# FFN input product of a two-layer transformer block: paired weight steps, so that matmuls of one width stand in runs of four steps in place of two

## The chip, the cores and the metric

The kernel runs on one core of a Trainium2 chip. The metric is the device time of one execution in microseconds (us). The profiled execution is one more execution, recorded by the hardware profiler.

## What is computed

Two decoder layers on 256 tokens of width 2048 in float32: attention mixers (left as they are by the change) and, in each layer, a feed-forward part whose first product is the subject:

```python
def conv_ffn(h, w_in, conv_w, conv_b, w_out):      # h: 256 x 2048, D_FF = 5632
    u = h @ w_in                                   # 2048 x 11264
    up = jnp.pad(u, ((0, 0), (CONV_WIDTH - 1, 0), (0, 0)))
    c = conv_b
    for j in range(CONV_WIDTH):
        c = c + conv_w[j] * up[:, j:j + s]
    g, val = c[..., :D_FF], c[..., D_FF:]
    return (jax.nn.gelu(g, approximate=True) * val) @ w_out
```

## The kernel before, in words

**High and low halves.** Float32 products are made from two parts of each operand, a rounded high part and the rest, the low part: high x high, high x low and low x high are added up in PSUM. For weights, ScalarE (ACT in rows) writes the high part `w_hi` from the landed weights `w_raw` (line 1315), and VectorE (DVE) then writes the low part `w_lo` (line 1903). I write hi(k) for TensorE's eight matmuls of step k with `w_hi`, and lo(k) for the eight with `w_lo`.

**Steps and slots.** A weight step is one load of 128 x 1024 weights (512 KB). `w_raw`, `w_hi` and `w_lo` have R = 4 slots each; step s uses slot s % 4. TensorE waits for `lo_ready` before a step, that is, for its low part (and so its high one, which VectorE reads). ScalarE may write the high part of step s once TensorE has added one to `step_used` for step s - 4. SyncE loads step s once `lo_ready` has come for step s - 4.

**Tiles.** In each layer the product is cut into 22 tiles of 512 output columns, by turns of the gate half and of the value half, with DSTEPS = 8 steps each. Even tiles use PSUM banks 0 to 3, odd ones banks 4 to 7. `merged_product` issues a tile: `both_halves` makes 8 matmuls of 512 columns (`w_hi` against both parts of x), `high_half` makes 8 of 256 columns (`w_lo` against the high part of x). Even steps go hi, lo; odd steps lo, hi. Tile 0 of a layer also carries transposes between its steps; tiles 1 to 20 are issued in a loop (line 1071), two in each turn, and tile 21 behind it.

**Epilogues.** While TensorE works on tile n, ScalarE and VectorE finish tile n - 1 in the gaps between splits, in an order written out by hand and the same in each loop turn: after the split of step 2 ScalarE copies PSUM (line 1704) as soon as the tile's last matmul is done, VectorE adds and scales it (lines 2413, 2415), and after the split of step 3 ScalarE makes the first convolution tap (line 1712); after the split of step 4 VectorE adds the other taps (line 2427, eight instructions), and the split of step 5 stands behind them. A gate half then gets its gelu (line 1721). Behind a value half, gate times value (line 2437) follows the split of step 5, the high part of the result `hT_hi` (line 1727) and its low part `hT_lo` (line 2443) follow that of step 6, and the splits of step 7 and of the next tile's step 0 stand behind them. So a tile during which a gate half is finished (odd tiles) and one during which a value half is finished (even tiles) differ; below they are the odd and the even tiles.

Of the kernel before, what the change touches and what calls it, by code (L numbers as in the profile page):

```python
# [22 lines left out]
P = 128  # L23
# [8 lines left out]
S = 256  # L32
# [17 lines left out]
R = 4  # L50
# [5 lines left out]
DSTEPS = KC // 2  # L56
LSTEPS = LORA // P // 2
FSTEPS = FC // 2
FJ = F // 512
# [89 lines left out]
def val(const, per, i):  # L149

    return const if i is None else i * per + const


def program(nc, x_in, mem_in, positions, inv_freq, w, vec, out):

    with ExitStack() as ctx:
        sem = lambda name: ctx.enter_context(nc.semaphore(name))
        base = 16512

        def at(name, shape, dt, offset):  # L160
            return nc.alloc_sbuf_tensor_at(name, shape, dt, offset=base + offset)
# [5 lines left out]
        xT = at("xT", [P, 2, KC, S], F32R, XT0)  # L167
        xT_hi, xT_lo = xT[:, 0], xT[:, 1]
        w_raw = at("w_raw", [P, R, 1024], F32, RING0)
        w_hi = at("w_hi", [P, R, 1024], F32R, RING0 + 16 * KB)  # L170
        w_lo = at("w_lo", [P, R, 1024], F32R, RING0 + 32 * KB)
# [120 lines left out]
        ps = ctx.enter_context(nc.psum_tensor("ps", [P, 8, 512], F32))  # L292
# [14 lines left out]
        step_used = sem("step_used")  # L307
# [192 lines left out]
        def _(pe):  # L500
            def release(tile_no, per=0, i=None):

                if tile_no >= 2:
                    pe.wait_ge(pair_act, val(tile_no - 1, per, i))
                    pe.wait_ge(pair_dve, val(tile_no - 1, per, i))
# [53 lines left out]
                    if turn_done:  # L559
                        turn_done(k, part_no)  # L560

            def merged_product(s0, tile_no, base, per=0, i=None, per_t=0, late=(), after=None):


                release(tile_no, per_t, i)
                for k in range(DSTEPS):
                    pe.wait_ge(lo_ready, val(s0 + k + 1, per, i))
                    for step, semaphore, value in late:
                        if k == step:
                            pe.wait_ge(semaphore, value)  # L570
                    slot = (s0 + k) % R
                    blocks = [(c, m4, slice(512 * c + P * m4, 512 * c + P * (m4 + 1)))
                              for c in range(2) for m4 in range(4)]
                    end = k == DSTEPS - 1

                    def both_halves(stop):
                        for c, m4, cols in blocks:
                            mm = nc.tensor.matmul(  # L578
                                ps[:, base + m4, :].rearrange("p (a n) -> p a n", a=2),
                                w_hi[:, slot, cols], xT[:, :, 2 * k + c, :], start=k == c == 0,  # L580
                                stop=stop and c == 1, skip_group_check=True)
                        return mm

                    def high_half(stop):
                        for c, m4, cols in blocks:
                            mm = nc.tensor.matmul(ps[:, base + m4, S:2 * S], w_lo[:, slot, cols],  # L586
                                                  xT_hi[:, 2 * k + c, :], start=False,
                                                  stop=stop and c == 1, skip_group_check=True)
                        return mm

                    if k % 2 == 0:
                        both_halves(False)
                        mm = high_half(end)
                    else:
                        high_half(False)
                        mm = both_halves(end)
                    mm.then_inc(step_used, 1)
                    if after:
                        after(k)

            whole = lambda n: (lambda a: a[:, 0:n])
            every = slice(0, S)
# [58 lines left out]
            def phase_free():  # L661

                if done["N"]:
                    pe.wait_ge(tr_lo, done["N"])
                if done["C"]:
                    pe.wait_ge(tr_copied, done["C"])
                if items_done[0]:
                    pe.wait_ge(o_lo, items_done[0])
# [20 lines left out]
            def x_transpose(g, tiles):  # L689

                return plain_transpose(x, g, tiles)

            def token_row(diag_no):

                pe.wait_ge(diag_ready, diag_no)
                pe.wait_ge(consts_ready, 2)
                nc.tensor.matmul(ps[:, 4, 0:S], ones[:, :],
                                 diag[:, :, :].rearrange("p t n -> p (t n)"), start=True,
                                 stop=True, skip_group_check=True).then_inc(tr_ready, 1)
# [11 lines left out]
            def unrotated_transpose(bank, buffer, rows, raw_no):  # L711

                pe.wait_ge(raw_ready, raw_no)
                for t in range(TT):
                    mm = nc.tensor.transpose(ps[:, bank, P * t:P * t + rows],
                                             pe_raw[0:rows, buffer, P * t:P * (t + 1)],
                                             ident[0:rows, 0:rows])
                mm.then_inc(unrotated, 1)
# [171 lines left out]
            def keep_busy(n, bank=WARM_BANK, block=ident_b[:, :]):  # L890

                for _ in range(n):
                    nc.tensor.matmul(ps[:, bank, 0:P], block, block, start=True, stop=True,  # L893
                                     skip_group_check=True)
# [74 lines left out]
            def beside_second(k):  # L969
# [3 lines left out]
                if k >= DSTEPS:  # L973
# [8 lines left out]
                    late=[(k, None, tr_lo, base_n + k + 1) for k in range(DSTEPS)])  # L982
# [5 lines left out]
                    after=lambda k: k == 1 and unrotated_transpose(6, 0, P, 1))  # L988
# [3 lines left out]
            for j in range(6):  # L992

                product(UQ + j * LSTEPS, LSTEPS, UQ_T + j, latq_hi, latq_lo, uq_parts(), width=384,
                        after=lambda k: k == 0 and j > 0 and
# [44 lines left out]
            def ffn_in(s_in, t_in, pieces, diag_no):  # L1040

                phase_free()
                pe.wait_ge(x_piece, pieces + 1)
                for g in range(4):
                    x_transpose(g, [0])
                pe.wait_ge(pair_act, t_in - 1)
                pe.wait_ge(pair_dve, t_in - 1)
                keep_busy(24, 2 * (t_in % 2))
                for g in range(4):
                    if g % 2 == 0:  # L1050
                        pe.wait_ge(x_piece, pieces + 3 + g // 2)
                    x_transpose(g, [1]).then_inc(tr_ready, 1)
                keep_busy(18, 2 * (t_in % 2))
                base_n = done["N"]
                done["N"] += DSTEPS
                done["C"] += 1
                tiles = lambda j, **kw: merged_product(s_in + j * DSTEPS, t_in + j, 4 * (j % 2), **kw)

                def between(k):
                    if k == 0:  # L1060
                        pe.wait_ge(x_piece, pieces + len(FFN_PIECES))
                    if k < 4:
                        x_transpose(4 + k, range(TT)).then_inc(tr_ready, 1)
                    if k == DSTEPS - 2:
                        token_row(diag_no)

                pe.wait_ge(pair_act, t_in)
                pe.wait_ge(pair_dve, t_in)
                tiles(0, late=[(k, tr_lo, base_n + k + 1) for k in range(DSTEPS)], after=between)
                pe.wait_ge(tr_copied, done["C"])  # L1070
                with pe.Fori(0, FJ - 1) as i:
                    for j in (1, 2):
                        tiles(j, per=2 * DSTEPS, i=i, per_t=2)
                tiles(2 * FJ - 1)

                h_count[0] += FJ
                pe.wait_ge(h_lo, h_count[0] - 1)

            pe.wait_ge(e_ready, T0_B - 2)
            for j in range(4):  # L1080
                product(OA + j * DSTEPS, DSTEPS, OA_T + j, xT_hi, xT_lo, n_parts(),
                        first_chunk=MEM_CHUNK, hold=HOLD if j % 2 else 0,
                        after=None if j else beside_oa0,
                        late=() if j else [(0, None, o_lo, T0_B - 7), (1, None, o_lo, T0_B - 3),
                                           (DSTEPS - 2, None, o_lo, T0_B - 2),
                                           (DSTEPS - 1, None, o_lo, T0_B)])
            ffn_in(IN0, IN0_T, PIECES_IN0, 4)

            def skv_transposes(k, part):
# [7 lines left out]
            for j in range(4):  # L1097
                product(OUT0 + j * FSTEPS, FSTEPS, OUT0_T + j, hT_hi, hT_lo, n_parts(),
                        late=[(FSTEPS - 2, None, h_lo, h_count[0])] if j == 0 else (),
# [132 lines left out]
            def beside_ob0(k):  # L1232
# [18 lines left out]
                if k == 4:  # L1251
# [10 lines left out]
                    late=[(h, None, tr_lo, base_n + h + 1) for h in range(BH)] +  # L1262
                    [(BH + k, None, o_lo, T0_B + BH + 2 * (k + 1)) for k in range(MH // 2)])
            pe.wait_ge(e_ready, T0_B + BH + MH)
            for j in range(1, 4):
                ob_tile(j)
            ffn_in(IN1, IN1_T, PIECES_IN1, 5)
            wide_product(OUT1, OUT1_T, FSTEPS, hT_hi, hT_lo,
                         [(FSTEPS - 2, None, h_lo, h_count[0])])
# [1350 lines left out]
```

## Time and profile before

| | us |
|---|---|
| median of 3 runs | 2195.57 (2195.2 to 2195.64) |
| profiled execution | 2196.11 |
| its span | 2194.3 |
| TensorE busy in the span | 2184.1 (100%) |
| VectorE busy | 1427.7 (65%) |
| ScalarE busy | 1225.1 (56%) |

The span runs from the first to the last recorded instruction; the execution's own time is 1.8 us longer. In the profile, PE is TensorE's matmuls, PEld its weight loads. The ends of matmuls are modelled, so distances between starts are what tells TensorE's pace.

### The profile page before, as it was taken

The page shows a single profiled execution, that of the slowest core. Times are in us where ns is not written, and L with a number is a line of the kernel's source. Part 1 is how long each engine was busy: PE and PEld are TensorE (multiplying, and loading weights), DVE is VectorE, ACT ScalarE, POOL GpSimd, SP SyncE. Part 2 cuts the span into 40 slices and gives each one's busy share as a digit, 9 for nine tenths or more (in the row PEclk, how much of TensorE's full clock was granted, in tenths as well). Part 3 has the DMA queues.
Part 4 walks back from the last instruction along what each step waited for, and adds up shares of the span by engine and source line. Part 5 has one row for each costly group of instructions (what it writes and reads, how often), then busy time and mean ns, then how long its engine had stood idle before and what let it go on. Part 6 is the DMA issues. An engine that isn't in the chain of part 4 may idle for free.

```text
span 2194.3 us, 33094 instructions
## 1 busy us (share of the span) xinstructions
PE 2184.1 (100%) x11835; PEld 1891.2 (86%) x11835; DVE 1427.7 (65%) x1938; ACT 1225.1 (56%) x1710; POOL 3.9 (0%) x16
## 2 busy tenths in 40 slices
PE   9999999999999999999999999999999999999998
PEld 8989988888888888888888888888888888888887
DVE  5666756777777777544476667567777776774444
ACT  5755655665656655443365567566566666554443
POOL 0000000000000000000000000000000000000000
PEclk9999999999999999999999999999999999999999
DMA  8665355556656666666656643656656666666664
GB/s 281 192 184 173 97 164 174 178 185 196 185 182 193 187 194 199 208 185 202 193 176 187 192 156 125 191 155 192 198 177 188 192 190 185 183 220 198 192 193 151
DMA packets 202737, 405.59 MB, mean 185 GB/s; under 512 B 12877, under 2 KB 16327, under 8 KB 201887
## 3 DMA queue, kind: packets, MB, share of 16 engines
q1 hardware_dynamic: 202079, 400.29, 58.7%
q0 software_dynamic: 576, 4.19, 0.5%
q8 instruction: 53, 0.87, 0.2%
q14 instruction: 29, 0.24, 0.0%
HBM read 402.34 MB, written 2.10 MB: 184 GB/s over the span
## 4 chain that ended last, share of the span: by engine, by line
PE 99%; DVE 0%; DMA 0%; ACT 0%; DVEq 0%; issue 0%
PE ps L548 43%; PE ps L578 29%; PE ps L586 15%; PE ps L616 3%; PE ps L626 3%; PE ps L1113 1%; PE ps L677 1%; PE ps L815 0%; PE ps L844 0%; PE ps L740 0%; PE ps L821 0%; PE ps L705 0%; PE ps L893 0%; PE ps L748 0%; PE ps L777 0%; DMA gain_rows<-in_gains 0%
## 5 line engine op out<-in xcount | busy, mean ns | idle before, releaser
L1903 DVE TENSOR_TENSOR w_lo<-w_raw,w_hi 128x1024 fp32r<-128x1024 f32 x608 | 736.9, 1223 | 480.1 <-ACT w_hi L1315 475.4
L1315 ACT ACTIVATE w_hi<-w_raw 128x1024 fp32r<-128x1024 f32 (+1 forms) x624 | 645.1, 1046 | 459.5 <-PE ps L548 324.3
L578 PE MATMUL ps<-xT,w_hi 128*128 128x512 f32 x2816 | 673.4, 391 | 0.1
L578 PEld LDWEIGHTS ps<-xT,w_hi 128*128 128x128 f32 x2816 | 517.0, 188 | 100.2 <-issue 0.4
L586 PEld LDWEIGHTS ps<-xT,w_lo 128*128 128x128 f32 x2816 | 361.6, 191 | 14.3 <-DVE w_lo L1903 0.4
L586 PE MATMUL ps<-xT,w_lo 128*128 128x256 f32 x2816 | 367.4, 283 | 0.0
L548 PE MATMUL ps<-w_hi,hT_hi 128*128 128x512 f32 x704 | 273.9, 389 | 0.0
L548 PE MATMUL ps<-w_hi,hT_lo 128*128 128x512 f32 x704 | 273.9, 389 | 0.0
L548 PE MATMUL ps<-w_lo,hT_hi 128*128 128x512 f32 x704 | 273.9, 389 | 0.0
L548 PE MATMUL ps<-w_hi,xT 128*128 128x512 f32 x640 | 203.0, 392 | 0.0
L548 PEld LDWEIGHTS ps<-w_lo,hT_hi 128*128 128x128 f32 x704 | 132.1, 188 | 27.6
L548 PEld LDWEIGHTS ps<-w_hi,hT_lo 128*128 128x128 f32 x704 | 132.1, 188 | 27.5
L548 PEld LDWEIGHTS ps<-w_hi,hT_hi 128*128 128x128 f32 x704 | 132.1, 188 | 27.1
L1890 DVE SCALAR_TENSOR_TENSOR w_lo<-w_raw,gcol,w_hi 128x512 fp32r<-128x512 f32 x160 | 111.4, 747 | 47.9 <-ACT w_hi L1311 47.7
L548 PEld LDWEIGHTS ps<-w_hi,xT 128*128 128x128 f32 x640 | 120.2, 188 | 24.5
L1311 ACT ACTIVATE w_hi<-w_raw,gcol 128x512 fp32r<-128x512 f32 x160 | 106.4, 719 | 59.8 <-PE ps L548 55.5
L548 PE MATMUL ps<-w_lo,xT 128*128 128x512 f32 x320 | 124.7, 390 | 0.0
L548 PE MATMUL ps<-w_hi,xbT_hi 128*128 128x512 f32 x256 | 100.6, 393 | 0.0
L548 PE MATMUL ps<-w_hi,xbT_lo 128*128 128x512 f32 x256 | 99.8, 390 | 0.0
L548 PE MATMUL ps<-w_lo,xbT_hi 128*128 128x512 f32 x256 | 99.6, 389 | 0.0
L1727 ACT ACTIVATE hT_hi<-scratch 128x1024 f32 x22 | 23.4, 1062 | 97.3 <-DVE scratch L2437 97.3
L2427 DVE SCALAR_TENSOR_TENSOR scratch<-u_value,conv,scratch 128x255 f32<-128x255 f32 (+1 forms) x176 | 73.3, 479 | 3.2
(285 smaller groups left out, 2145.4 us busy)
## 6 DMA issues: line engine op xcount, KB each, us to landing
w_raw<-in_ffn_w_in SPq DMA_DIRECT2D x352, 512.0 KB, 4.1
w_raw<-in_ffn_w_out SPq DMA_DIRECT2D x176, 512.0 KB, 4.6
w_raw<-in_shared_w_kv SPq DMA_DIRECT2D x48, 512.0 KB, 4.0
w_raw<-in_a_w_o SPq DMA_DIRECT2D x32, 512.0 KB, 4.7
w_raw<-in_b_w_in SPq DMA_DIRECT2D x32, 512.0 KB, 4.7
w_raw<-in_b_w_o SPq DMA_DIRECT2D x32, 512.0 KB, 4.6
w_raw<-in_a_w_mem_kv SPq DMA_DIRECT2D x16, 512.0 KB, 6.9
w_raw<-in_b_w_mem_kv SPq DMA_DIRECT2D x16, 512.0 KB, 4.4
```

The costliest lines, as they stand in the source:

```text
L548: mm = nc.tensor.matmul(dst, st, mv, start=first and q == 0, stop=last and q == len(pairs) - 1, skip_group_check=True)
L578: mm = nc.tensor.matmul(ps[:, base + m4, :].rearrange("p (a n) -> p a n", a=2), w_hi[:, slot, cols], xT[:, :, 2 * k + c, :], start=k == c ...
L586: mm = nc.tensor.matmul(ps[:, base + m4, S:2 * S], w_lo[:, slot, cols], xT_hi[:, 2 * k + c, :], start=False, stop=stop and c == 1, skip_gr ...
L616: mm = nc.tensor.matmul(ps[:, bank, 256 * (h % 2):256 * (h % 2) + S], wk[:, P * h:P * (h + 1)], xk, start=bank not in begun, stop=False, s ...
L626: mm = nc.tensor.matmul(ps[:, bank, :], xk[:, tok_t[t]], wk[:, KV_HEADS * P:2 * KV_HEADS * P], start=bank not in begun, stop=False, skip_g ...
L677: mm = nc.tensor.transpose(ps[:, bank, o0:o0 + P], src[:, t, f0:f0 + P], ident[:, :])
L1311: a = nc.scalar.activation(w_hi[:, s % R, cols], w_raw[:, s % R, cols], ACT.Copy, scale=gcol[:, row:row + 1])
L1315: nc.scalar.activation(w_hi[:, s % R, 0:width], w_raw[:, s % R, 0:width], ACT.Copy)\
L1727: nc.scalar.activation(hT_hi[:, bass.ds(i * 4, 4), :], scratch[:, 1], ACT.Copy).then_inc(h_hi, 1)
L1890: d = nc.vector.scalar_tensor_tensor(out=w_lo[:, s % R, cols], in0=w_raw[:, s % R, cols], scalar=gcol[:, row:row + 1], in1=w_hi[:, s % R, ...
L1903: nc.vector.tensor_tensor(w_lo[:, s % R, :], w_raw[:, s % R, :], w_hi[:, s % R, :].bitcast(F32), ALU.subtract)\
L2427: d = nc.vector.scalar_tensor_tensor(out=c, in0=u, scalar=conv[:, layer, 2 - shift, bass.ds(ch, 1)], in1=c, op0=ALU.mult, op1=ALU.add)
```

## The change

`merged_product` gets a parameter `paired`. With it, the steps are taken two at a time: the first kind of both steps, then the second kind of both steps; the next pair begins with the kind that the last one ended with. The loop (tiles 1 to 20) and tile 21 are paired, 42 tiles over two layers; tile 0 keeps its order. Each step has its own wait, ahead of its first kind, and its own signal `step_used`, behind its second kind.

```diff
-            def merged_product(s0, tile_no, base, per=0, i=None, per_t=0, late=(), after=None):
+            def merged_product(s0, tile_no, base, per=0, i=None, per_t=0, late=(), after=None, paired=False):
...
-                    if k % 2 == 0:
-                        both_halves(False)
-                        mm = high_half(end)
-                    else:
-                        high_half(False)
-                        mm = both_halves(end)
-                    mm.then_inc(step_used, 1)
-                    if after:
-                        after(k)
+
+                run = 2 if paired else 1
+                for k0 in range(0, DSTEPS, run):
+                    steps = range(k0, k0 + run)
+                    first, second = both_halves, high_half
+                    if k0 // run % 2:
+                        first, second = high_half, both_halves
+                    for k in steps:
+                        ready(k)
+                        first(k)
+                    for k in steps:
+                        second(k).then_inc(step_used, 1)
+                        if after:
+                            after(k)
...
-                        tiles(j, per=2 * DSTEPS, i=i, per_t=2)
-                tiles(2 * FJ - 1)
+                        tiles(j, per=2 * DSTEPS, i=i, per_t=2, paired=True)
+                tiles(2 * FJ - 1, paired=True)
```

`ready(k)` holds the waits that stood ahead of each step before, and `both_halves(k)`, `high_half(k)` the same matmuls as before.

TensorE's order at the start of the loop body (the first tile of a turn) in layer 0, before; `ps` is PSUM, `w_hi` and `w_lo` the split weights, `xT` the transposed x, and a row with `waits lo_ready` opens a step:

```order
L567 ISA [waits pair_dve,pair_act]
L578 MATMUL ps<-xT,w_hi 128x512 [waits lo_ready]
L578 MATMUL ps<-xT,w_hi 128x512 x7
L586 MATMUL ps<-xT,w_lo 128x256 x8
L567 REGISTER_ALU
L586 MATMUL ps<-xT,w_lo 128x256 [waits lo_ready]
L586 MATMUL ps<-xT,w_lo 128x256 x7
L578 MATMUL ps<-xT,w_hi 128x512 x8
L567 REGISTER_ALU
L578 MATMUL ps<-xT,w_hi 128x512 [waits lo_ready]
```

The same place of the changed kernel:

```order
L588 ISA [waits pair_dve,pair_act]
L570 MATMUL ps<-xT,w_hi 128x512 [waits lo_ready]
L570 MATMUL ps<-xT,w_hi 128x512 x7
L588 REGISTER_ALU
L570 MATMUL ps<-xT,w_hi 128x512 [waits lo_ready]
L570 MATMUL ps<-xT,w_hi 128x512 x7
L581 MATMUL ps<-xT,w_lo 128x256 x16
L588 REGISTER_ALU
L581 MATMUL ps<-xT,w_lo 128x256 [waits lo_ready]
L581 MATMUL ps<-xT,w_lo 128x256 x7
L588 REGISTER_ALU
L581 MATMUL ps<-xT,w_lo 128x256 [waits lo_ready]
```

The wait for step 1 has moved ahead of lo(0), to stand eight 512-column matmuls into the tile; that for step 3 stands eight 256-column matmuls behind that for step 2. A tile's order was hi 0, lo 0, lo 1, hi 1, hi 2, lo 2, lo 3, hi 3, hi 4 and so on; it is now hi 0, hi 1, lo 0, lo 1, lo 2, lo 3, hi 2, hi 3, hi 4, hi 5, lo 4, lo 5, lo 6, lo 7, hi 6, hi 7. The orders of the other engines are unchanged.

## Rows read from the trace of the kernel before

**Rows 1.** The page: busy time and share of TensorE; its granted clock; the ending chain by line.

```profile
PE 2184.1 (100%) x11835; PEld 1891.2 (86%) x11835; DVE 1427.7 (65%) x1938; ACT 1225.1 (56%) x1710; POOL 3.9 (0%) x16
...
PEclk9999999999999999999999999999999999999999
...
PE ps L548 43%; PE ps L578 29%; PE ps L586 15%; PE ps L616 3%; PE ps L626 3%; PE ps L1113 1%; PE ps L677 1%; PE ps L815 0%; PE ps L844 0%; PE ps L740 0%; PE ps L821 0%; PE ps L705 0%; PE ps L893 0%; PE ps L748 0%; PE ps L777 0%; DMA gain_rows<-in_gains 0%
```

**Rows 2.** Timeline of TensorE's matmuls, 480 to 508 us: start, us, engine, line, operation, count.

```profile
481.80 3.82 PE L578 MATMUL ps<-xT,w_hi 128*128 128x512 f32 x16
485.46 2.08 PE L586 MATMUL ps<-xT,w_lo 128*128 128x256 f32 x16
487.37 3.82 PE L578 MATMUL ps<-xT,w_hi 128*128 128x512 f32 x16
...
504.07 3.82 PE L578 MATMUL ps<-xT,w_hi 128*128 128x512 f32 x16
507.72 2.08 PE L586 MATMUL ps<-xT,w_lo 128*128 128x256 f32 x16
```

**Rows 3.** Line 1704, 439 to 862 us: count, duration in ns, first and last start.

```profile
L1704 ACT ACTIVATE u_gate<-ps x10: 1029/1029/1029, 439.3 to 840.1; 128x1024 f32<-128x1024 f32 x10
```

**Rows 4.** Line 548's matmuls, 900 to 950 us, 512 columns, three groups by turns.

```profile
L548 PE MATMUL ps<-w_lo,hT_hi x74: 389/389/389, 899.8 to 949.4; 128*128 128x512 f32 x74
...
L548 PE MATMUL ps<-w_hi,hT_hi x74: 389/389/389, 900.3 to 949.9; 128*128 128x512 f32 x74
```

**Rows 5.** Line 548's matmuls, 162 to 178 us, 256 columns, two groups by turns.

```profile
L548 PE MATMUL ps<-xT,w_hi x91: 283/283/283, 161.8 to 178.0; 128*128 128x256 f32 x91
L548 PE MATMUL ps<-xT,w_lo x45: 283/283/283, 162.0 to 177.8; 128*128 128x256 f32 x45
```

**Rows 6.** Timeline of ScalarE and VectorE in an odd tile, 483 to 500 us.

```profile
483.84 1.03 ACT L1704 ACTIVATE u_gate<-ps 128x1024 f32<-128x1024 f32 x1 [1.69 <-PE ps L578]
...
486.16 1.22 DVE L2415 TENSOR_TENSOR u_gate<-u_gate,rstd_row 128x1024 f32<-128x1024 f32 x1
487.31 1.22 DVE L1903 TENSOR_TENSOR w_lo<-w_raw,w_hi 128x1024 fp32r<-128x1024 f32 x1
487.63 2.08 ACT L1712 ACTIVATE scratch<-u_gate,conv 128x256 f32<-128x256 f32 x4 [1.82 <-DVE u_gate L2415]
489.62 1.99 ACT L1315 ACTIVATE w_hi<-w_raw 128x1024 fp32r<-128x1024 f32 x2
490.69 1.23 DVE L1903 TENSOR_TENSOR w_lo<-w_raw,w_hi 128x1024 fp32r<-128x1024 f32 x1 [2.17 <-ACT w_hi L1315]
491.84 3.47 DVE L2427 SCALAR_TENSOR_TENSOR scratch<-u_gate,conv,scratch 128x255 f32<-128x255 f32 x8
...
495.22 4.84 DVE L1903 TENSOR_TENSOR w_lo<-w_raw,w_hi 128x1024 fp32r<-128x1024 f32 x4
```

**Rows 7.** Timeline of ScalarE and VectorE in an even tile, 517 to 524 us.

```profile
517.42 1.22 DVE L1903 TENSOR_TENSOR w_lo<-w_raw,w_hi 128x1024 fp32r<-128x1024 f32 x1
...
519.91 1.06 ACT L1727 ACTIVATE hT_hi<-scratch 128x1024 f32 x1 [4.41 <-DVE scratch L2437]
...
521.13 1.23 DVE L2443 TENSOR_TENSOR hT_lo<-scratch,hT_hi 128x1024 f32 x1 [0.21 <-ACT hT_hi L1727]
522.27 2.35 DVE L1903 TENSOR_TENSOR w_lo<-w_raw,w_hi 128x1024 fp32r<-128x1024 f32 x2
```

**Rows 8.** Timeline of tile 1 in layer 0: matmuls, VectorE, weight loads.

```profile
392.47 3.82 PE L578 MATMUL ps<-xT,w_hi 128*128 128x512 f32 x16
...
407.26 2.34 PE L586 MATMUL ps<-xT,w_lo 128*128 128x256 f32 x16
409.44 3.82 PE L578 MATMUL ps<-xT,w_hi 128*128 128x512 f32 x16
...
407.10 3.49 DVE L1903 TENSOR_TENSOR w_lo<-w_raw,w_hi 128x1024 fp32r<-128x1024 f32 x3
...
408.38 1.01 PEld L586 LDWEIGHTS ps<-xT,w_lo 128*128 128x128 f32 x8 [0.21 <-DVE w_lo L1903]
```

More of the change, by code:

```diff
@@ L560, in product, with both_halves, high_half, ready @@
                         turn_done(k, part_no)
-            def merged_product(s0, tile_no, base, per=0, i=None, per_t=0, late=(), after=None):
+            def merged_product(s0, tile_no, base, per=0, i=None, per_t=0, late=(), after=None, paired=False):
                 release(tile_no, per_t, i)
-                for k in range(DSTEPS):
+                def both_halves(k):
+                    for c in range(2):
+                        for m4 in range(4):
+                            cols = slice(512 * c + P * m4, 512 * c + P * (m4 + 1))
+                            mm = nc.tensor.matmul(
+                                ps[:, base + m4, :].rearrange("p (a n) -> p a n", a=2),
+                                w_hi[:, (s0 + k) % R, cols], xT[:, :, 2 * k + c, :],
+                                start=k == c == 0, stop=k == DSTEPS - 1 and c == 1,
+                                skip_group_check=True)
+                    return mm
+                def high_half(k):
+                    for c in range(2):
+                        for m4 in range(4):
+                            cols = slice(512 * c + P * m4, 512 * c + P * (m4 + 1))
+                            mm = nc.tensor.matmul(ps[:, base + m4, S:2 * S],
+                                                  w_lo[:, (s0 + k) % R, cols],
+                                                  xT_hi[:, 2 * k + c, :], start=False, stop=False,
+                                                  skip_group_check=True)
+                    return mm
+                def ready(k):
                     pe.wait_ge(lo_ready, val(s0 + k + 1, per, i))
@@ L570, in merged_product @@
                             pe.wait_ge(semaphore, value)
[L571 to L589, printed above, removed]
-                    if k % 2 == 0:
-                        both_halves(False)
-                        mm = high_half(end)
-                    else:
-                        high_half(False)
-                        mm = both_halves(end)
-                    mm.then_inc(step_used, 1)
-                    if after:
-                        after(k)
+                run = 2 if paired else 1
[11 more added lines that the diff above has]
+                            after(k)
             whole = lambda n: (lambda a: a[:, 0:n])
```

## The prediction

> **What bounds the kernel now.** I read the page first: TensorE is busy 2184.1 of 2194.3 us, its granted clock is full (the 2.4 GHz level) in all 40 slices, and the ending chain runs through its matmuls, the FFN input product's two lines holding 29% and 15% [rows 1]. Nothing that another engine saves can show; what counts is the distance between TensorE's starts, and waits that it does not have today.
>
> Then the timeline of one tile [rows 2]. A run of 16 matmuls of 512 columns holds the engine for 485.46 - 481.80 = 3.66 us, one of 16 of 256 columns for 487.37 - 485.46 = 1.91 us. The tile boundary lies in the middle of the first run. The copy of the finished tile starts every second tile, 10 times in 439.3 to 840.1 us: 400.8 / 18 = 22.267 us a tile [rows 3]. I call the start of a tile's first matmul T and give times as T + something. In a long stretch of one width, 222 matmuls of 512 columns (74 of each of three groups) start between 899.8 and 949.9 us, 50.1 / 221 = 0.2267 us each [rows 4], and 136 of 256 columns between 161.8 and 178.0, 16.2 / 135 = 0.120 us [rows 5].
>
> **What the order saves.** A tile of 64 + 64 matmuls at those paces would last 64 x 0.2267 + 64 x 0.120 = 22.19 us; it lasts 22.267. The missing 0.078 us are four rounds of width changes, 0.0195 each: by the rows a 512 run after a change has 3.66 where 16 x 0.2267 = 3.63, and a 256 run 1.91 where 1.92. The change leaves two rounds in a tile in place of four. Two layers have 42 paired tiles: 84 rounds x 0.0195 = 1.64 us saved. The bounds: nothing, if the excess were bound to the count of matmuls, and 1.64 if to the changes. I take 1.64, since runs of one width, 222 long, show none of it. A paired tile then lasts 22.23 us.
>
> Here a rule speaks. The Trainium skill, TensorE: Matmul & The Clock Gate, section "Back-to-back issue gap", gives the distance of matmuls as their columns over the clock plus a small constant, whatever stands ahead; by it nothing would be saved and the sum below would be 5.4 in place of 3.7. The rows disagree in the small: the same 16 matmuls take 3.66 us behind the other width and 3.63 inside a long run.
>
> **What moves: the waits.** No instruction is added; TensorE asks for some steps earlier. With the paces above, hi(0) and hi(1) take 16 x 0.2267 = 3.63, lo(0) to lo(3) 1.91 + 16 x 0.120 = 3.83, hi(2) to hi(5) 3.66 + 3.63 = 7.28, lo(4) to lo(7) 3.83. First matmuls of each step, before and after:
>
> step 1: T + 2.77, now T + 1.81. Step 3: T + 8.33, now T + 3.63 + 0.95 + 0.96 + 0.96 = T + 6.50. Step 5: T + 13.92, now T + 3.63 + 3.83 + 3.66 + 1.81 = T + 12.93. Step 7: T + 19.48, now T + 3.63 + 3.83 + 7.28 + 0.95 + 1.92 = T + 17.61. Steps 0, 2, 4 and 6 keep their starts within 0.1 us (step 6: T + 16.70, now T + 16.65).
>
> Against that stands when VectorE has the low part. Odd tile, T = 481.80 + 1.84 = 483.64 (half of the run of 3.66, whose second half is 8 x 0.2267 = 1.81) [rows 2]. The copy starts at T + 0.20, directly behind the last matmul; add and scale end at 487.38; the first tap runs 487.63 to 489.71 and holds ScalarE, so the high parts of steps 4 and 5 come from 489.62 on; the low part of 4 runs to 491.92, the eight other taps fill 491.84 to 495.31, and the low part of 5 runs 495.22 to 495.22 + 1.22 = 496.44 = T + 12.80 [rows 6]. That of step 3 ends at 488.53 = T + 4.89, well before T + 6.50. Nothing in this chain waits for slots: it hangs on T alone. Slots do come free later, since hi(0) and hi(1) stand ahead of lo(0): step 0's at T + 4.6 in place of T + 2.8, but ScalarE is held until T + 5.98 by the tap; step 2's at T + 9.3 in place of T + 8.3, for step 6, whose low part VectorE can't begin ahead of 496.3 = T + 12.7 anyway. This costs nothing. Without the tap's cover step 4's low part would come some 2.5 us behind the slot, at T + 7, against T + 11.11. The four low parts from 495.22 on (steps 5, 6, 7 and the next 0) end at 500.06 = T + 16.42, so in odd tiles 6 and 7 are in time.
>
> Even tile, T = 504.07 + 1.84 = 505.91 [rows 2]. The low part of step 5 ends at 517.42 + 1.22 = 518.64 = T + 12.73. The low part of step 7 must wait for gate times value, for `hT_hi` (519.91) and for `hT_lo` (521.13): it is the first of the two that begin at 522.27, and ends at 523.49 = T + 17.58 [rows 7]. Step 6's stands ahead of `hT_lo`, so it is done by T + 15.22, in time. It is asked for at T + 17.61 now; before, it had 1.9 us to spare.
>
> **What a late step costs.** One wait of this kind stands in the trace, in tile 1: the low part of step 5 is the first of three that begin at 407.10 and ends at 407.10 + 1.22 = 408.32, the weight load follows at 408.38, and lo(5) should have begun at 407.26 + 0.95 = 408.21. The run took 409.44 - 407.26 = 2.18 in place of 1.91, so it began 0.27 late, at 408.48 [rows 8]. So a matmul can start 0.16 us after VectorE's end: 0.06 to the load and 0.10 for it. Lateness is end + 0.16 - start asked for.
>
> Odd tiles 3 to 21, step 5: 12.80 + 0.16 - 12.93 = 0.03 by these rounded rows; the chain's end varies by some hundredths of a us from tile to tile, I take 0.04. 20 tiles: 0.8 us.
> Even tiles, step 5: 12.73 + 0.16 = 12.89, in time by 0.04. Step 7: 17.58 + 0.16 - 17.61 = 0.13. 20 tiles: 2.6 us.
> Tile 1: T = 392.47 + 1.84 = 394.31, and the low part of step 5 ends at T + 14.01, since its chain starts late behind tile 0. 14.01 + 0.16 - 12.93 = 1.24, of which 0.27 are paid already: 0.97 more, two layers 1.94 us [rows 8].
>
> A late step doesn't grow: the copy of the tile waits for TensorE, and the chain starts anew at each T. Queued behind the waiting load are all matmuls of the step; ScalarE and VectorE have their next free slot later by the same lateness, covered as above.
>
> Sum: -1.64 + 0.8 + 2.6 + 1.94 = +3.7 us. The profiled 2196.11 would become 2199.8; it is 0.54 above the median, so the median 2195.57 becomes 2199.3, +0.17%. What a measurement of this kernel can tell from no change I put at 0.2%, 4.4 us: the sum ends 0.7 us short of it.
>
> Unknown is a late load in the middle of a 512 run, which no row shows. Lower bound: it costs as in the 256 run, or nothing where a long matmul still runs. Upper bound: the run's pace starts anew, 0.03 more in each of 22 odd tiles (+0.7), or the case of the first rival. I take the lower, being nearest to the one wait that has a row, and keep 4.4 as that far end. The 0.16 could be wrong by 0.02 either way: 42 x 0.02 = 0.8.
>
> **Rivals.**
> 1. A late load can't overlap the matmul in flight. At step 5 the load is asked for after the last matmul of hi(4) has started; if it has to wait for that one's end, hi(5) begins 0.10 to 0.11 late in every odd tile in place of 0.04: 20 x 0.07 = 1.4 more. In even tiles step 5 would be late too, but step 7 then less so, no net cost. Sum 5.1: 2200.7, slower by 0.23%. It decides from 0.035 more in each odd tile. For it: no row shows a load that begins midway in a 512 matmul. Against: in 256 runs load and matmul overlap all the time. The Trainium skill, TensorE: Matmul & The Clock Gate, section "Step-by-step: what each phase is for", has weight loads go ahead of matmuls in flight, which also speaks against it; no row here has the case. Chance 0.16.
> 2. The 0.16 belongs to tile 1, and elsewhere a step is ready some 0.03 after VectorE's end. Then odd and even tiles have no wait, tile 1 pays 0.8 more twice: -1.64 + 1.7 = 0, 2195.6. For it: there is only one such wait in each layer. Against: load and its length are the same everywhere. Chance 0.16.
> 3. The rounds aren't saved, the waits come: +5.4, 2200.9, slower. Only the excess being tied to something else, such as each step's wait or signal, would do it; the long stretches have these too and no excess. Chance 0.05.
> 4. Faster by over 0.2%: would need 4.4 us, more than twice what all saved rounds hold, with no wait at all. 0.03.
>
> **How the numbers follow.** My own case has 0.60: around 2199.3 with -1.0 to +1.5; some 0.13 of it lies beyond 4.4 us. Same: 0.47 + 0.16 = 0.63. Slower: 0.13 + 0.16 + 0.05 = 0.34. Faster 0.03. The range takes in my case and the dearer rivals, 2197.2 to 2201.6; it leaves out the second rival, most of the 2 in 10.
>
> **What would show it.** In the profile after: 32 matmuls of 256 columns in one timeline row and the next run 3.83 us on; 7.28 us for 32 of 512 columns. In even tiles weight loads of the 256-column line that wait for the low part, some 20 times, 0.13 us later at step 7; the copies of line 1704 at alternating distances of 22.27 (odd) and 22.36 (even), 44.63 for two. In tile 1, hi(5) 1.24 us late. Wrong would be the whole if no load waits for VectorE (rival 2), if odd tiles last 22.34 (rival 1), or if TensorE's pace within a long run differs from 0.2267 and 0.120.

## The result

| | before | changed |
|---|---|---|
| median, us | 2195.61 (18 runs, 2195.2 to 2197.33) | 2199.59 (18 runs, 2199.17 to 2200.8) |
| ratio | | 1.0018, 95% interval 1.0011 to 1.0024 |
| span of the profiled execution | 2194.3 | 2197.6 |

The changed kernel is 4.0 us slower, 0.18%; 2199.3 had been forecast. The interval is 2.4 to 5.3 us and clear of zero. Three views of it answer to the rows of before. First the page, TensorE's busy time and the ending chain (lines have moved by a few: 570 is the high part's matmul, 581 the low part's, 1909 VectorE's split, 1710 the copy of a finished tile, 2433 the other taps):

```profile
PE 2184.4 (99%) x11835; PEld 1888.1 (86%) x11835; DVE 1427.3 (65%) x1938; ACT 1224.3 (56%) x1710; POOL 3.9 (0%) x16
...
PE 98%; DVE 1%; ACT 1%; issue 0%; DMA 0%; DVEq 0%; ACTq 0%; SPq 0%
```

The page of before has for the chain:

```profile
PE 99%; DVE 0%; DMA 0%; ACT 0%; DVEq 0%; issue 0%
```

TensorE is busy as long as before [rows 1]; what is new is that VectorE and ScalarE hold 1% each of the chain that ends last. The copies of finished tiles, line 1710, first and last start over twenty tiles:

```profile
L1710 ACT ACTIVATE u_gate<-ps x10: 1029/1029/1029, 439.7 to 841.4; 128x1024 f32<-128x1024 f32 x10
```

401.7 / 9 = 44.63 us for two tiles, where before 400.8 / 9 = 44.53 [rows 3]. TensorE's timeline, an odd tile and the even one behind it:

```profile
483.66 4.24 PE L570 MATMUL ps<-xT,w_hi 128*128 128x512 f32 x18
487.74 4.00 PE L581 MATMUL ps<-xT,w_lo 128*128 128x256 f32 x32
491.57 7.51 PE L570 MATMUL ps<-xT,w_hi 128*128 128x512 f32 x32
498.92 3.99 PE L581 MATMUL ps<-xT,w_lo 128*128 128x256 f32 x32
...
510.03 4.00 PE L581 MATMUL ps<-xT,w_lo 128*128 128x256 f32 x32
513.87 7.45 PE L570 MATMUL ps<-xT,w_hi 128*128 128x512 f32 x32
521.15 4.12 PE L581 MATMUL ps<-xT,w_lo 128*128 128x256 f32 x32
525.11 5.18 PE L570 MATMUL ps<-xT,w_hi 128*128 128x512 f32 x22
```

Distances between starts are what is read here. The 32 low-part matmuls of steps 0 to 3 hold the engine 3.83 us, as worked out. The 32 high-part ones of steps 2 to 5 hold it 513.87 to 521.15 = 7.28 in the even tile, but 491.57 to 498.92 = 7.35 in the odd one: 0.07 lost at step 5. The low-part ones of steps 4 to 7 hold it 525.11 - 521.15 = 3.96 in the even tile, 0.13 over the 3.83: that is step 7. The weight loads of the odd tile's step 5 name what they waited for; the last row, from the weight loads' waits between 416 and 864 us (tiles 2 to 21 of the first layer), says that 10 loads did so, one for each odd tile (total, times and longest, us):

```profile
495.69 2.36 DVE L1909 TENSOR_TENSOR w_lo<-w_raw,w_hi 128x1024 fp32r<-128x1024 f32 x2
...
496.97 0.53 PEld L570 LDWEIGHTS ps<-xT,w_hi 128*128 128x128 f32 x3 [0.19 <-DVE w_lo L1909]
...
PEld ps L570 <- DVE w_lo L1909: 1.9, 10, 0.2
```

The low part of step 5 ends at 495.69 + 1.22 = 496.91 (1.22 is one split's time), and the load begins 0.06 later, as in the one wait of before [rows 8]. With T = 487.74 - 3.63 = 484.11 that end is T + 12.80, where it was before: the other engines' chain did hang on T alone. For step 7 of the even tile, VectorE's row is

```profile
522.78 2.35 DVE L1909 TENSOR_TENSOR w_lo<-w_raw,w_hi 128x1024 fp32r<-128x1024 f32 x2
```

The first of the two ends at 524.00, while the step is asked for at 521.15 + 0.95 + 1.92 = 524.02; with the 0.16 from VectorE's end to the matmul it is 0.14 late. The view of the waits names no load of line 581, although the prediction looked for some 20 of them in the even tiles: the load stands still for less than 0.1 us there, too short to be named. Tile 1:

```profile
401.05 5.63 PE L570 MATMUL ps<-xT,w_hi 128*128 128x512 f32 x24
407.65 2.14 PE L570 MATMUL ps<-xT,w_hi 128*128 128x512 f32 x8 [0.98 <-DVE w_lo L1909]
409.63 3.98 PE L581 MATMUL ps<-xT,w_lo 128*128 128x256 f32 x32
```

Here steps 2 to 5 hold the engine 409.63 - 401.05 = 8.58 in place of 7.28: 1.30 us, of which 0.27 were there before, at the same step.

The spans differ by 3.3 us and the medians by 4.0. The rest lies ahead of the product, in code that is the same. The high part's matmuls of both layers, first and last start, before and changed:

```profile
L578 PE MATMUL ps<-xT,w_hi x2816: 387/389/481, 369.7 to 1946.9; 128*128 128x512 f32 x188
L570 PE MATMUL ps<-xT,w_hi x2816: 387/389/504, 369.0 to 1950.2; 128*128 128x512 f32 x188
```

From the first to the last that is 1577.2 us before and 1581.2 changed, 4.0 more.

### The profile page after: what moved, and what is told of

Same layout as the page of the kernel before. It is cut to its first block, busy times and chain, and to the rows that moved or that the text cites. A ratio compares the mean times of both kernels' runs of the same rounds, so it can differ in the third digit from the quotient of the medians.

```text
span 2197.6 us, 33094 instructions
## 1 busy us (share of the span) xinstructions
PE 2184.4 (99%) x11835; PEld 1888.1 (86%) x11835; DVE 1427.3 (65%) x1938; ACT 1224.3 (56%) x1710; POOL 3.9 (0%) x16
## 4 chain that ended last, share of the span: by engine, by line
PE 98%; DVE 1%; ACT 1%; issue 0%; DMA 0%; DVEq 0%; ACTq 0%; SPq 0%
PE ps L548 43%; PE ps L570 28%; PE ps L581 15%; PE ps L622 3%; PE ps L632 3%; PE ps L1119 1%; PE ps L683 1%; PE ps L821 0%; PE ps L850 0%; PE ps L746 0%; PE ps L827 0%; PE ps L711 0%; PE ps L754 0%; DVE scratch L2433 0%; PE ps L783 0%
## 5 line engine op out<-in xcount | busy, mean ns | idle before, releaser
L570 PE MATMUL ps<-xT,w_hi 128*128 128x512 f32 x2816 | 659.7, 391 | 2.0 <-DVE w_lo L1909 2.0
L581 PEld LDWEIGHTS ps<-xT,w_lo 128*128 128x128 f32 x2816 | 351.4, 191 | 8.5
L581 PE MATMUL ps<-xT,w_lo 128*128 128x256 f32 x2816 | 355.9, 284 | 0.0
L2433 DVE SCALAR_TENSOR_TENSOR scratch<-u_gate,conv,scratch 128x255 f32<-128x255 f32 (+1 forms) x176 | 73.2, 478 | 3.1
```

What stands on the lines that cost most here:

```text
L570: mm = nc.tensor.matmul(ps[:, base + m4, :].rearrange("p (a n) -> p a n", a=2), w_hi[:, (s0 + k) % R, cols], xT[:, :, 2 * k + c, :], start ...
L581: mm = nc.tensor.matmul(ps[:, base + m4, S:2 * S], w_lo[:, (s0 + k) % R, cols], xT_hi[:, 2 * k + c, :], start=False, stop=False, skip_grou ...
L2433: d = nc.vector.scalar_tensor_tensor(out=c, in0=u, scalar=conv[:, layer, 2 - shift, bass.ds(ch, 1)], in1=c, op0=ALU.mult, op1=ALU.add)
```

## The experiments

Each kernel was timed beside the kernel before, on the same chip as it. Lines are those of the changed kernel unless said.

**The waits taken away (e1).** The paired order stays. In the epilogue loop the other taps go behind the split of step 5, and ScalarE's `hT_hi` and VectorE's two operations on the value half behind the next split each:

```diff
 # VectorE
-                            if ahead == 5:
+                            if ahead == 6:
                                 other_taps(i, j)
-                            if ahead == 6 and j == 1:
+                            if ahead == 7 and j == 1:
                                 gate_times_value(i)
-                            if ahead == 7 and j == 1:
+                            if ahead == 8 and j == 1:
                                 lo_half(i)
 # ScalarE
-                            if ahead == 7 and j == 1:
+                            if ahead == 8 and j == 1:
                                 hi_half(i)
```

> Theory (the change saves two width changes a tile, 0.02 us each, and gives more back because low parts come late for step 5 in odd tiles and step 7 in even ones): with the low part of step 5 ahead of the other taps, and that of step 7 ahead of the low part of the result, no load of weights waits, paired tiles last 22.23 us each (now 22.29 and 22.35, before 22.27), and the median is 2195.6 - 1.6 - 0.5 (tile 1's old wait) = 2193.5. Rival (late waits are real, but the width changes save nothing): tiles of 22.27, 2195.1. Rival (the loss is not in these waits): 2199 or so, as the changed kernel.

Measured: 2193.47 us (11 runs, 2193.07 to 2194.63), ratio to before 0.9989, interval 0.998 to 0.9998. The timelines of TensorE and of VectorE in it, over the odd tile that begins at 482.56 us (found as before, from TensorE's runs: 486.19 - 16 x 0.2267):

```profile
481.65 4.70 PE L570 MATMUL ps<-xT,w_hi 128*128 128x512 f32 x20
486.19 4.00 PE L581 MATMUL ps<-xT,w_lo 128*128 128x256 f32 x32
490.02 7.44 PE L570 MATMUL ps<-xT,w_hi 128*128 128x512 f32 x32
497.30 4.00 PE L581 MATMUL ps<-xT,w_lo 128*128 128x256 f32 x32
501.13 7.22 PE L570 MATMUL ps<-xT,w_hi 128*128 128x512 f32 x31
```

```profile
489.62 2.36 DVE L1909 TENSOR_TENSOR w_lo<-w_raw,w_hi 128x1024 fp32r<-128x1024 f32 x2 [2.18 <-ACT w_hi L1321]
491.89 3.48 DVE L2433 SCALAR_TENSOR_TENSOR scratch<-u_gate,conv,scratch 128x255 f32<-128x255 f32 x8
```

3.83, 7.28, 3.83 us: no run is longer than its matmuls. The low parts of steps 4 and 5 come one behind the other, both done by 491.98 = T + 9.42, and the eight taps fill the time after. The copies over twenty tiles:

```profile
L1710 ACT ACTIVATE u_gate<-ps x10: 1029/1029/1029, 438.3 to 838.4; 128x1024 f32<-128x1024 f32 x10
```

400.1 / 9 / 2 = 22.23 us a tile. Both halves of the theory are in this run: with no wait a paired tile is shorter than one of before by 0.04, and the waits were all that stood against it. The rivals gave 2195.1 and 2199. The interval alone, which reaches up to 2195.3, would not exclude the first; tiles of 22.23 in place of 22.27 do.

**The epilogue's order alone (e2).** The same edit on the kernel before.

> The order of matmuls of before with the epilogue order of e1. Theory: only tile 1's wait of 0.27 us in each layer goes, 2195.1, tiles of 22.27. Rival (the reordered epilogue is what makes e1 faster): as fast as e1, 2193.5.

Measured: 2195.09 us (11 runs, 2194.74 to 2196.13), ratio 0.9995, interval 0.9986 to 1.0004; here the copies go from 438.7 to 839.5, 22.27 a tile. By the medians the reordering is worth 0.6 us without pairing and 6.2 with it (from +4.0 to -2.2); the interval alone would not tell the 0.6 from nothing. The profile's tile times do not change, and what is gone from its weight loads' waits is the pair of the kernel before that waited for `w_lo`, tile 1's in each layer.

**One kind of tile at a time (e3, e4).** Odd tiles, then even tiles paired:

```diff
-                        tiles(j, per=2 * DSTEPS, i=i, per_t=2, paired=True)
+                        tiles(j, per=2 * DSTEPS, i=i, per_t=2, paired=j == 1)   # e3; e4: j == 2
```

In e4 tile 21, which is odd, isn't paired either.

> Only odd tiles paired. Theory (each tile's chain starts anew at its own first matmul): odd tiles 22.29, even tiles 22.27, tile 1 longer by 0.98: 20 x 0.025 + 2 x 0.98 = +2.5 us, 2198.1. Rival (lateness is handed on from tile to tile through the slots that come free late): odd tiles behind an unpaired one are not late, 22.23, and the total is below +1.2 us.

> Only even tiles paired. Theory: even tiles 22.35, odd 22.27, tile 1 as before: 20 x 0.08 = +1.6 us, 2197.2; with the odd ones' +2.5 that makes the whole +4.1. Rival (handed on): even tiles not late, 22.23, 2194.8.

Measured: e3 2198.37 us (11 runs, 2197.92 to 2200.61), ratio 1.0012, interval 1.0003 to 1.0022; e4 2197.08 us (11 runs, 2196.94 to 2199.98), ratio 1.0008, interval 0.9999 to 1.0017. The kernel before had a median of 2195.72 beside them: +2.65 and +1.36, together +4.0, the whole loss. By its interval e4 could be nothing; its tiles say that it isn't. The line of copies in e3 and in e4:

```profile
L1710 ACT ACTIVATE u_gate<-ps x10: 1029/1029/1029, 439.8 to 840.8; 128x1024 f32<-128x1024 f32 x10
```

```profile
L1710 ACT ACTIVATE u_gate<-ps x10: 1029/1029/1029, 438.7 to 840.2; 128x1024 f32<-128x1024 f32 x10
```

401.0 / 9 = 44.56 and 401.5 / 9 = 44.61 for two tiles; less the 22.27 of an unpaired one that is 22.29 for an odd and 22.34 for an even paired tile. So a tile is late by itself, and the slots that come free later in the paired tile ahead have no part in it. Odd tiles cost more in total (+2.65) though each is hardly longer, because of tile 1.

**More rounds, no earlier step (e5).** In the 42 tiles every step goes high, low; no pairing:

```diff
-                run = 2 if paired else 1
+                run = 1
...
-                    if k0 // run % 2:
+                    if not paired and k0 % 2:
                         first, second = high_half, both_halves
```

> The 42 tiles with high then low in every step: eight rounds of width changes a tile in place of the four of before, no step asked for earlier. Theory (a round costs 0.0195 us however many matmuls stand in it): tiles of 22.267 + 4 x 0.0195 = 22.345, 168 rounds more, +3.3 us, 2198.9, and no load that waits. Rival (the excess is tied to steps or signals, not to width changes): 2195.6, tiles of 22.27.

Measured: 2198.83 us (11 runs, 2198.3 to 2201.69), +3.0 on the 2195.86 beside it, ratio 1.0015, interval 1.0006 to 1.0024. Its rows:

```profile
482.82 2.00 PE L570 MATMUL ps<-xT,w_hi 128*128 128x512 f32 x8
484.67 1.12 PE L581 MATMUL ps<-xT,w_lo 128*128 128x256 f32 x8
485.62 2.00 PE L570 MATMUL ps<-xT,w_hi 128*128 128x512 f32 x8
```

A run of 8 of 512 columns holds the engine 1.85 us where 8 x 0.2267 = 1.81, one of 256 columns 0.95 where 0.96, and the copies go from 438.3 to 840.6, 402.3 / 18 = 22.35 us a tile. With e1's 22.23 (two rounds) and before's 22.27 (four) that makes 0.02 us a round over two, four and eight rounds.

**One more instruction in front of the low part of step 5 (e6).**

```diff
                             if ahead == 5:
                                 other_taps(i, j)
+                                nc.vector.reduce_sum(stat[:, 0, 0:1], rstd_row[:, :], axis=AX)
```

> The changed kernel with one more VectorE instruction of about 0.3 us (a sum whose result nothing reads) behind the other taps in each tile, ahead of the low part of step 5. Theory (TensorE has no slack at those steps): each of the 42 tiles lengthens by the instruction's time, 42 x 0.3 = +12.6 us on the changed kernel, 2212. Rival (a late low part is partly absorbed, since the matmul in flight covers it): under half of that, below 2206.

Measured: 2215.51 us (4 runs, 2214.71 to 2217.28), ratio 1.0091, interval 1.0076 to 1.0107; +19.65 on the 2195.86 beside it, so 15.7 above the changed kernel. VectorE's timeline shows what it was given:

```profile
494.27 3.47 DVE L2433 SCALAR_TENSOR_TENSOR scratch<-u_gate,conv,scratch 128x255 f32<-128x255 f32 x8
497.66 0.42 DVE L2461 TENSOR_REDUCE stat<-rstd_row 128x1 f32<-128x256 f32 x1
497.99 2.35 DVE L1909 TENSOR_TENSOR w_lo<-w_raw,w_hi 128x1024 fp32r<-128x1024 f32 x2
```

The sum puts the split off by 497.99 - 497.66 = 0.33 us, and 42 x 0.33 = 13.9. It is more than the expected 12.6 by 3.1: 1.3 from the instruction's length, and the other 1.8 from elsewhere. The copies, in the first layer and in the second, show where most of that lies:

```profile
L1710 ACT ACTIVATE u_gate<-ps x10: 1029/1029/1029, 440.9 to 849.5; 128x1024 f32<-128x1024 f32 x10
L1710 ACT ACTIVATE u_gate<-ps x10: 1029/1029/1029, 1535.7 to 1943.4; 128x1024 f32<-128x1024 f32 x10
```

Two tiles last 408.6 / 9 = 45.40 us in the first layer, 0.77 more than 44.63, but 407.7 / 9 = 45.30 in the second, where the excess is the 0.66 by which two splits were put off. In the first layer's even tiles VectorE stands idle 0.33 us before `hT_lo`, in the second's 0.22, and step 7 is late by that much more; why is open. The rival is out: TensorE has no slack at these steps.

**Runs of eight steps (e7).** One round a tile: pairs become groups of four steps (`run = 4`), and the epilogue is laid around it, with the taps behind the split of step 3, the gelu, `hT_hi` and gate times value behind that of step 7, and `hT_lo` behind the next one:

```diff
-                run = 2 if paired else 1
+                run = 4 if paired else 1
...
-                            if ahead == 5:
+                            if ahead == 4:
                                 other_taps(i, j)
```

> One round of width changes a tile in place of two: first kind of four steps, then second kind of four steps, with an epilogue order that keeps the splits of steps 4 to 7 together behind the other taps. Saved against e1: 42 x 0.0195 = 0.8 us, if nothing comes late. Theory: the slot of step 0 comes free only at T + 8.2 and steps 4 to 7 are then asked for every 0.96 us from T + 11.1 on, while VectorE takes 1.14 for each low part; step 4 would be just in time and steps 6 and 7 0.2 to 0.5 us late, in each of 42 tiles: 8 to 20 us more than e1, 2202 to 2213. Rival (longer runs pay further): 2192.7.

Measured: 2211.56 us (5 runs, 2210.98 to 2211.71), ratio 1.0071, interval 1.0057 to 1.0084, 18 us above e1. TensorE and VectorE in it:

```profile
482.82 9.68 PE L570 MATMUL ps<-xT,w_hi 128*128 128x512 f32 x42
492.34 8.26 PE L581 MATMUL ps<-xT,w_lo 128*128 128x256 f32 x64
500.43 7.90 PE L570 MATMUL ps<-xT,w_hi 128*128 128x512 f32 x34
```

```profile
491.30 3.47 DVE L2433 SCALAR_TENSOR_TENSOR scratch<-u_gate,conv,scratch 128x255 f32<-128x255 f32 x8 [1.34 <-ACT scratch L1718]
494.69 4.62 DVE L1909 TENSOR_TENSOR w_lo<-w_raw,w_hi 128x1024 fp32r<-128x1024 f32 x4
```

The 64 low-part matmuls hold the engine 8.09 us where 64 x 0.12 = 7.67: four splits take 4.62 us, 1.14 from one to the next, and TensorE would use a step's low part every 0.96. A longer run asks for low parts faster than VectorE makes them, for 0.02 us saved.

## Why the prediction was right

**What the order saves.** Forecast 1.64 us from 84 rounds of 0.0195; e1's tiles of 22.23 and e5's of 22.35 show the size and that it goes with the number of rounds. The Trainium skill, TensorE: Matmul & The Clock Gate, section "Back-to-back issue gap", gives for a matmul by itself, at the full clock, the columns over 2.4 plus 2.5 ns, in which the matmul ahead has no part. By such a rule the tiles of e1, e5 and the kernel before would be of one length. The runs decide against it in this small term; the measured distances, 226.7 and 120.0 ns, are also above 216 and 109 ns, an estimate from its figures.

**Where the waits come.** Step 5 in odd tiles, step 7 in even ones and step 5 of tile 1 were named, from the ends of VectorE's low parts and starts worked out from TensorE's two paces. All three are there, and e1 removes them and the loss.

**Their sizes.** The even tiles' step 7 was forecast at 0.13; the rounded rows have 0.13, e4's twenty tiles 22.34 - 22.23, about 0.12. Tile 1: forecast 0.97 more for the wait, measured 1.30 - 0.27 = 1.03. Odd tiles: forecast 0.04, measured 0.07 in the one tile shown and 0.06 by e3's twenty. Here the term "an unknown late load in the middle of a 512 run" was mis-sized: the lower bound was taken, and the case lies near that of the upper one (0.03 more). That the run's pace starts anew is argued from this size, which is that of the excess behind a change of width, 3.66 against 3.63.

The forecast for two tiles, 22.27 + 22.36 = 44.63 us, was met to the hundredth by 22.29 + 22.34: the odd term was too small and the even one too large by about the same, and that much is luck. Over the kernel the odd tiles' excess is some 0.4 us and tile 1's 0.1, the even tiles' shortfall 0.2. The medians can't tell a loss of 3.7 from one of 4.0, since the interval spans 2.9 us; which waits there are, and roughly how long, rests on the traces.

**What could be told.** The prediction put at 0.2% what a measurement can tell from no change, and gave 0.63 to a loss below that. The loss was below it, 0.18%, but with 18 runs of each kernel the interval is 0.11 to 0.24%: smaller losses can be told than was assumed.

**Two slips in the working.** Step 5 was asked for before at T + 13.90, not T + 13.92. The second rival's sum takes 0.8 us for tile 1, where by its own terms the 0.97 stays; it gives 2195.9, not 2195.6. Neither changes an argument.

**The rivals.** That a late load can't overlap the matmul in flight asked for odd tiles of 22.34; e3 has 22.29. That the 0.16 us belongs to tile 1 alone asked for no wait elsewhere, and the ten odd tiles behind tile 1 have one each. Rounds not saved, and a gain, are out with e1 and the result.

**Argued only.** That the excess at a change of width is a property of TensorE's queue or of its array no run tells; only its size and where it stands are shown. Width, weights and the columns of PSUM written all change together there. The weights and the moving operand also change from matmul to matmul in the long stretch of one width, which shows no excess [rows 4], so they alone don't make it; the PSUM columns no run has tried.

## What to carry to other kernels

When a change reorders work on the engine that sets the time, write down for each wait the time at which it is now asked for, and beside it when its producer is done in the trace: here 0.04 us were gained per tile. Against that 0.06 and 0.12 us were lost in odd and even tiles, where the producer had had 0.9 and 1.7 us to spare and the new order used all of it, and 1.03 more in tile 1, where it had been late already. A loss of this kind may be the other engine's order and not the change: moving the eight taps and three operations on the value half behind one more split each turned +4.0 us into -2.2. And longer runs of one kind ask for one input in bursts, so the producer's pace within a burst (1.14 against 0.96 us a step) bounds their length.

## What the runs showed of the hardware

- At a granted clock of 0.999, matmuls of 512 columns start every 0.2267 us (222 in a row) and of 256 every 0.120 (136 in a row). One round trip between the two widths costs 0.02 us whether 8 (e5), 16 (before) or 32 matmuls (e1) stand in a run: tiles of 22.35, 22.27 and 22.23 us.
- A weight load that waits for VectorE's low part begins 0.06 us after its end, before a matmul of 512 columns (changed kernel, 496.91 to 496.97) as before one of 256 (kernel before, 408.32 to 408.38).
- In the 256 run, the matmul starts 0.16 us after VectorE's end. In the 512 run, what the run loses is that and some 0.03 us more (0.07 where 0.03 to 0.04 were worked out; in tile 1 1.30 where 1.24).
